# Mixture of experts on one core: three unequal lanes in the third pass, outputs scattered by assignment, first weights fetched during routing

## The reference

```python
choice = scores + router_bias                      # scores: sigmoid of a 64-wide product
_, top_e = lax.top_k(jnp.where(emask, choice, -jnp.inf), MOE_TOPK)     # 8 per token, from 4 of 8 groups
gw = gw / jnp.sum(gw, axis=-1, keepdims=True) * ROUTED_SCALE
...
def step(y, blk):                                  # blk: up to 128 tokens of one expert
    tok, wt, e = blk
    out = swiglu(hf[tok], exp_gate[e], exp_up[e], exp_down[e])         # 1024 -> 2 x 256 -> 1024
    return y.at[tok].add(out.astype(F32) * wt[:, None]), None
...
shared = swiglu(hf, sh_gate, sh_up, sh_down)
x = x + g2 * (y + shared); return rms_norm_2(x, final_g)
```

## Time and profile before

| | us |
|---|---|
| median of 3 runs (lowest, highest) | 2332.45 (2327.95, 2344.47) |
| profiled execution | 2335.72 |
| its span, first to last instruction | 2333.9 |
| PE busy in the span | 2148.9 (92%) |
| DVE busy | 1328.9 (57%) |
| POOL busy | 398.1 (17%) |
| DMA moved in the span | 446.34 MB, mean 191 GB/s |

### The profile page before, as it was taken

How to read it: one execution, slowest core, us unless ns; L and a number is a source line. 1 busy time by engine, 2 the same in 40 slices (tenths; PEclk the granted TensorE clock), 3 DMA queues, 4 the chain that set the end, 5 groups by cost and what they waited for, 6 DMA issues and landing times. The chain is left out here.

```text
span 2333.9 us, 27568 instructions
## 1 busy us (share of the span) xinstructions
PE 2148.9 (92%) x10379; PEld 1246.9 (53%) x10379; DVE 1328.9 (57%) x2524; ACT 461.0 (20%) x915; POOL 398.1 (17%) x771
## 2 busy tenths in 40 slices
PE   6999989999999999999879999998699999999976
PEld 3444654877785458883443788445333333333322
DVE  3448953766672134434968343535766767766756
ACT  2013561221110011004235232011011111111121
POOL 0005000112000000000000000000344444444524
PEclk9999999999999999999989999998899999999998
DMA  9412100545524015981111100401499989899977
GB/s 393 178 76 82 37 3 21 232 156 209 212 82 180 37 73 233 390 306 54 37 55 61 51 3 2 180 36 54 163 373 394 424 351 417 341 406 387 385 280 296
DMA packets 69142, 446.34 MB, mean 191 GB/s; under 512 B 12291, under 2 KB 12947, under 8 KB 44209
## 3 DMA queue, kind: packets, MB, share of 16 engines
q0 software_dynamic: 36176, 254.42, 27.2%
q1 hardware_dynamic: 32866, 190.52, 21.1%
HBM read 416.01 MB, written 73.45 MB: 210 GB/s over the span
## 5 line engine op out<-in xcount | busy, mean ns | idle before, releaser
L965 PE MATMUL psum<-arena 128*128 128x256 f32 x1904 | 416.3, 380 | 2.1 <-PEq L1005 2.1
L2824 PE MATMUL psum<-arena 128*64 128x512 f32 (+1 forms) x1088 | 367.4, 603 | 39.6 <-DVE arena L2872 16.8
L965 PEld LDWEIGHTS psum<-arena 128*128 128x128 f32 x1904 | 361.4, 190 | 62.3 <-issue 13.7
L2872 DVE STREAM_TRANSPOSE arena<-arena 32x256 f32<-32x256 f32 x832 | 362.2, 435 | 16.0 <-DMA arena<-scratch_h,arena 4.3
L2824 PEld LDWEIGHTS psum<-arena 128*64 128x64 f32 (+1 forms) x1088 | 144.7, 166 | 227.3 <-issue 201.4
L2815 PE MATMUL psum<-arena 128*64 128x512 f32 (+1 forms) x544 | 186.2, 598 | 1.2 <-ACT arena L2850 1.2
L1067 PE MATMUL psum<-arena 128*128 128x512 f32 x352 | 151.8, 592 | 0.3 <-PEq L1091 0.3
L2815 PEld LDWEIGHTS psum<-arena 128*64 128x64 f32 (+1 forms) x544 | 68.5, 163 | 113.2 <-issue 111.8
L869 PE MATMUL psum<-arena 128*128 128x512 f32 x256 | 113.7, 603 | 2.3 <-DVE arena L2432 1.5
L1067 PEld LDWEIGHTS psum<-arena 128*128 128x128 f32 x352 | 66.6, 190 | 83.4 <-issue 83.4
L2878 DVE COPY arena<-psum 128x512 f32<-128x512 f32 x51 | 35.3, 692 | 132.3 <-PE psum L2815 132.3
(11 more groups left out here) (520 smaller groups left out, 2925.3 us busy)
## 6 DMA issues: line engine op xcount, KB each, us to landing
scratch_expert_out<-arena SPq DMA_DIRECT2D x18, 2048.0 KB, 19.9
scratch_expert_out<-arena SPq DMA_DIRECT2D x51, 512.0 KB, 9.0
arena<-in_w_ada SPq DMA_DIRECT2D x12, 2048.0 KB, 16.2
arena<-in_ada_w POOLq DMA_DIRECT2D x12, 2048.0 KB, 8.8
arena<-in_w_up SPq DMA_DIRECT2D x22, 1024.0 KB, 4.8
arena<-in_w_in SPq DMA_DIRECT2D x9, 2048.0 KB, 10.8
arena<-in_w_down SPq DMA_DIRECT2D x5, 2048.0 KB, 8.3
arena<-in_w_o SPq DMA_DIRECT2D x2, 2048.0 KB, 8.5
```

The costliest lines, as they stand in the source:

```text
L965: last = pe.matmul(out, w[:, k, :], x[:, k, :], start=(k == 0), stop=(k == KH - 1))
L2824: last = pe.matmul(K.bank[2 + s][r, :], xt[:, s, P * k + r.start:P * k + r.stop], gu[:, lane, 2 * E_FF * k:2 * E_FF * (k + 1)], start=(k = ...
L2872: last = dve.transpose(channels[c:c + 32, :, a:a + 32], tokens[a:a + 32, :, c:c + 32])
```

## The change

The diff, cut to its core. The routing arithmetic on DVE is rewritten for three kinds of blocks (full; remainders of 33 to 64 rows; of 1 to 32 rows); it has about as many steps as before and is not shown but for the number of trips. `K.asg` lists the assignment of each row (token x 8 + rank), and `K.tok` comes from it by a shift, one more step at the end of the chain.

```diff
-LANES, LANE = 4, 32
+LANES, LANE = 5, 32
# phase_in2, sync: the fill of expert_out is gone
-                fill(3)
-            fill(len(parts))
-            sp.wait_ge(filled.sem, filled.n)
# phase_route, vector: ends = running sums of (full, 64-row, 32-row); RC_SHARE = 1, 2/3, 2/5; RC_TWOS = 0, 2, 4, ...
+            step(stt(out=num[:, 4:7], in0=ends[:, :, last], scalar=-0.5, in1=const[:, RC_SHARE:RC_SHARE + 3], op0=ALU.add, op1=ALU.mult))
+            step(dve.tensor_reduce(most, num[:, 4:7], AX.X, ALU.max))
+            step(ts(trips[:, :], const[:, RC_TWOS:RC_TWOS + LANE], most, None, ALU.is_lt))
+            step(dve.tensor_reduce(N, trips[:, :], AX.X, ALU.add))
# phase_route, gpsimd: after the sources are ready, first weights of three lanes and one down
+            for to, src, col_, landed in ((K.gu_lane[0], gu_rows, 0, K.gu_in[0]), (K.down_lane[0], down_rows, LANES, K.down_in[0]),
+                                          (K.gu_lane[1], gu_rows, 1, K.gu_in[1]), (K.gu_lane[2], gu_rows, 2, K.gu_in[2])):
+                offset = bass.IndirectOffsetOnAxis(ap=K.wrows[:, col_:col_ + 1], axis=0)
+                pool.indirect_dma_start(to, None, src, offset, bounds_check=EXPERTS * P - 1, oob_is_err=False).then_inc(landed.sem, 16)
...
# phase_experts
-    halves = lambda s: [(slice(0, P), s)] if s < 2 else [(slice(0, 64), 2), (slice(64, P), 3)]
+    tiles = lambda s: [(slice(0, P), s)] if s < 2 else [(slice(0, 64), 2), (slice(64, 96), 3), (slice(96, P), 4)]
# tensor: down product and gate/up product
                 for k in range(KD):
-                    for r, lane in halves(s):
+                    for r, lane in tiles(s):
                         last = pe.matmul(K.bank[2 + s][r, :], xt[:, s, P * k + r.start:P * k + r.stop],
-                                         gu[:, lane, 2 * E_FF * k:2 * E_FF * (k + 1)], start=(k == 0), stop=(k == KD - 1))
+                                         gu[lane][:, 2 * E_FF * k:2 * E_FF * (k + 1)], start=(k == 0), stop=(k == KD - 1))
# tensor, ahead of the loop: the first block's rows are turned here; ACT and DVE copy half each
+            pe.wait_ge(x_in[0].sem, 16)
+            for k in range(KD):
+                last = pe.transpose(K.bank[k // 4][:, P * (k % 4):P * (k % 4) + P], xg[:, 0, P * k:P * k + P], K.ident[:, :])
+            first_turned.by(last)
# gpsimd: no memset; down weights are fetched one step later than gate/up; a block is scattered four steps later
-            link(pool, pool.memset(xg[:, :, :], 0.0), cleared)
+            def scatter(i, s, off):
+                b = (s + off) % U
+                blocks_done(pool, out_act, i, s, off)
+                blocks_done(pool, out_dve, i, s, off)
+                pool.tensor_copy(out_rows[:, b:b + 1], K.asg[:, at(i, s + off)]).then_inc(out_step.sem, 1)
+                blocks_done(pool, out_step, i, s, off)
+                pool.tensor_tensor(wait_for[:, 6:7], K.rstd[:, 0:1], K.rstd[:, 0:1], ALU.add)
+                pool.indirect_dma_start(d["expert_out"], bass.IndirectOffsetOnAxis(ap=out_rows[:, b:b + 1], axis=0), out[:, b, :], None,
+                                        bounds_check=T * TOP - 1, oob_is_err=False).then_inc(out_dma[b].sem, 16)
...
+                gather(i, s, 1)
+                fetch_gu(i, s, lanes_of(s))
+                if not (isinstance(i, int) and U * i + s == U):
+                    fetch_down(i, s - 1)
+                if not isinstance(i, int) or U * i + s >= LAG:
+                    scatter(i, s, -LAG)
...
# sync: the plain store is gone; phase_combine: SP loads plain rows, all four tiles, no ring
-                dst = d["expert_out"][at(i, s)].rearrange("a p n -> (a p) n")
-                sp.dma_start(dst, out[:, s, :]).then_inc(out_dma[s].sem, 16)
+    ON_DVE, PARTS = 3, ((3, 5), (5, 8), (0, 3))
+            def load(t):
+                rows = d["expert_out"][P * TOP * t:P * TOP * (t + 1)].rearrange("(p j) n -> p j n", j=TOP)
+                for n, (lo, hi) in enumerate(PARTS):
+                    part_in[t][n].by(sp.dma_start(yg[t][:, lo:hi, :], rows[:, lo:hi, :]), 16)
```

More of the change, by code:

```diff
@@ L2613, in _ @@
             stt = dve.scalar_tensor_tensor
-            scan = lambda to, x: step(dve.tensor_tensor_scan(to[:, :], ones[:, :], x[:, :], 0.0, ALU.mult, ALU.add))
+            flat = lambda x: x.rearrange("p a e -> p (a e)")
             last = EXPERTS - 1
[L2616 to L2651, removed]
@@ L2660, in _ @@
[L2660 to L2664, removed]
+            N, most, widest = (num[:, m:m + 1] for m in range(3))
+            place_at, V, gone, found = num[:, 8:15], num[:, 15:16], num[:, 16:17], num[:, 17:18]
@@ new lines, in _ @@
+            V2, found2 = num[0:LANE, 18:19], num[0:LANE, 19:20]
+            full, fend, all_full = kinds[:, 0, :], ends[:, 0, :], ends[:, 0, last:]
+            step(tt(raised[:, :, :], cnt.unsqueeze(1).to_broadcast([P, 3, EXPERTS]), const[:, RC_UP:RC_UP + 3].unsqueeze(2).to_broadcast([P, 3, EXPERTS]), ALU.add))
+            step(ts(flat(raised[:, :, :]), flat(raised[:, :, :]), BLOCK.bit_length() - 1, None, ALU.logical_shift_right))
+            step(dve.tensor_copy(flat(kinds[:, :, :]), flat(raised[:, :, :])))
@@ new lines, in _ @@
+            step(dve.tensor_reduce(most, num[:, 4:7], AX.X, ALU.max))
+            step(ts(trips[:, :], const[:, RC_TWOS:RC_TWOS + LANE], most, None, ALU.is_lt))
+            step(dve.tensor_reduce(N, trips[:, :], AX.X, ALU.add))
+            step(stt(out=widest, in0=ends[:, 1, last:], scalar=all_full, in1=N, op0=ALU.subtract, op1=ALU.max))
+            vector = lambda m: const[:, RC_PLACE + 7 * m:RC_PLACE + 7 * m + 7]
+            step(stt(out=place_at, in0=vector(0), scalar=N, in1=vector(1), op0=ALU.mult, op1=ALU.add))
@@ new lines, in _ @@
+            step(stt(out=hat[:, :], in0=first_tail[:, :], scalar=at_(6), in1=got[:, :], op0=ALU.add, op1=ALU.add))
+            for m in (1, 2):
+                step(ts(got[:, :], first_tail[:, :], at_(m), at_(3 + m), ALU.is_gt, ALU.mult))
+                step(tt(hat[:, :], hat[:, :], got[:, :], ALU.add))
+            step(tt(base[:, :], fend, full, ALU.subtract))
+            step(tt(jump[:, :], hat[:, :], fend, ALU.subtract))
+            step(tt(jump[:, :], jump[:, :], tail[:, :], ALU.mult))
@@ L2686, in _ @@
             sf = slot_f[:, :, :].rearrange("p t j -> p (t j)")
[L2687 to L2696, removed]
+            step(stt(out=num[:, 20:28], in0=const[:, RC_BEYOND:RC_BEYOND + 8], scalar=N, in1=const[:, RC_BEYOND + 8:RC_BEYOND + 16], op0=ALU.mult, op1=ALU.add))
+            for lane in range(1, LANES):
+                to = again[:, 0:NT * TOP] if lane > 1 else beyond[:, :]
+                step(ts(to, sf, num[:, 19 + lane:20 + lane], num[:, 23 + lane:24 + lane], ALU.is_gt, ALU.mult))
+                if lane > 1:
+                    step(tt(beyond[:, :], beyond[:, :], to, ALU.add))
             link(dve, stt(out=K.slot[:, :], in0=sf, scalar=-1.0, in1=beyond[:, :], op0=ALU.add, op1=ALU.add), slots_done)
@@ L2813, in down_products @@
                     for k in range(2):
-                        for r, lane in halves(b):
+                        for r, lane in tiles(b):
                             last = pe.matmul(K.bank[5 + half][r, :], ht[:, b, P * k + r.start:P * k + r.stop],
-                                             down[:, lane, D * k + 512 * half:D * k + 512 * half + 512], start=(k == 0), stop=(k == 1))
+                                             down[lane][:, D * k + 512 * half:D * k + 512 * half + 512], start=(k == 0), stop=(k == 1))
                 last.then_inc(down_mm.sem, 1)
@@ L2909, in gather, with fetch @@
                                         bounds_check=T - 1, oob_is_err=False).then_inc(x_in[b].sem, 16)
-            def load(i, s, used, to, src, index, ready, landed_):
-                blocks_done(pool, used, i, s, -U)
+            def fetch(i, at, lanes, used, to, src, index, ready, landed_):
+                trip, last = at // U, lanes[-1] + 1
+                blocks_done(pool, used, i, at, -U)
                 pool.tensor_tensor(wait_for[:, 5:6], K.rstd[:, 0:1], K.rstd[:, 0:1], ALU.add)
-                for _, lane in halves(s):
-                    col_ = bass.ds(i + LANE * lane, 1) if not isinstance(i, int) else slice(LANE * lane + i, LANE * lane + i + 1)
+                for lane in lanes:
+                    n = LANE * lane + trip
+                    col_ = bass.ds(i + n, 1) if not isinstance(i, int) else slice(i + n, i + n + 1)
@@ L2916, in load @@
                     pool.tensor_copy(wrows[:, index + lane:index + lane + 1], K.source[:, col_]).then_inc(ready.sem, 1)
-                done = s + 1 if s < U - 1 else LANES
-                pool.wait_ge(ready.sem, LANES * i + done if isinstance(i, int) else i * LANES + done)
+                pool.wait_ge(ready.sem, LANES * (i + trip) + last if isinstance(i, int) else i * LANES + (LANES * trip + last))
```

(19 more changed lines are left out.)

220 lines of the change are left out of this document (130 added, 90 removed).

## The result

The changed kernel takes 2437.1 us (median of 4 runs, 2434.3 to 2438.1) against 2335.5: ratio 1.043, 95% interval 1.0409 to 1.0451. It is slower by 101.6 us, where 104 were forecast.

What follows compares the result with a forecast made beforehand. PE was taken to set the pace, with DMA nearly full. Fifteen trips of 45.9 us (689) replace 17 of 33.9 (576); with start, +2 and -6.5 at the end, +104 gives 2437 us, range 2280 to 2475.

Steps and rivals of the forecast that it cites:

- The deciding term: Third block: each width change costs 0.14 us and nothing overlaps across it; +13.4 us a trip.
- Trips: Expert loop: 15 trips instead of 17, at 45.9 us instead of 33.9; weight loads rise to 63.
- DMA and POOL under it: Expert loop: DMA's 42 us and POOL's at most 34 us a trip stay under 45.9; PE alone sets the pace.
- the 1.4 us: Expert loop: the time PE loses per trip in the kernel before, claimed to go once PE alone sets the pace.
- Start: Start of the expert stage: 2.4 + 4.2 us gained, some 6 us earlier; third block at 1698.
- 7.3 MB (17 us at 430) fit in: Routing: early weight transfers fit into DMA's idle time between 1641.9 and 1660 us.
- the sign named for the start: Expert stage: the start is right if the first gate/up begins about 1671.
- The terms that were named: Stage start: gather loses 2.7 us memset, gains 0.3 us step (2.4); turning the first rows takes 3 us, not 7.2 (4.2).
- End: After the last down product: scatter adds 2 us, plain loads bring the last stage's first join 6.5 us earlier.
- +2 and -6.5: Kernel's end: +2 us for the scatter's POOL work, -6.5 us for the first join at about 2283 through plain loads.
- Sum: Whole kernel: last down product at 2370 instead of 2262, everything moves by +104, span 2438, median 2437 us.
- The first rival: Third block: three widths run together at no price, DMA decides in front; 2293 us, chance 0.28.

Runs made afterwards that it cites:

- grouping: Changed kernel, third block taking all steps k of the 64-row lane first, then those of the two 32-row lanes: 2400.4 us, ratio 1.0268.
- 23.1 MB less: Changed kernel with lane 4's weights not moved from the third trip on: 2434.8 us, ratio to before 1.0432.
- mixed widths: Kernel before, with the second 64-row half of the third block as two tiles of 32 columns: 2533.5 us, ratio 1.0842.
- equal tiles: Changed kernel with the third block taken in four 32-column tiles: 2322.9 us, ratio to before 0.9943.
- the fill: Changed kernel with 8 of the 18 scratch fill transfers put back, and the wait at the end of SP's list: 2437.1 us, ratio 1.043.
- the three with less: Changed kernel without early weight fetch during routing (2446.4 us), with 5.2 of its 7.3 MB (2436.3), and the latter with four 32-column tiles (2323.3).

## Why the prediction was right

**The deciding term** was the third block, and it came out as worked: 16.0 and 8.0 us forecast, 15.95 and 8.01 measured, a change 0.14 against 0.134. The reason was right too, and not only the size: the same tiles without a second width lose it (2322.9), the kernel before gains it by a second width alone (2533.5), and grouping separates its two parts. The rule of the Trainium skill (TensorEngine Tiling (Array Packing), Key Properties) that a change of tiling mode drains the engine agrees with the weight loads of the changed kernel, where 32-column weights enter 1.0 us after the 64-column ones, when both passes are over.

**Trips.** 15, as counted; 45.4 us each, not 45.9. The working rounded a step of 1.98 to 2.0 and took 32.5 - 10.6 = 21.9 for the rest of a trip, which is 21.6: 6.6 us in 14 trips.

**DMA and POOL under it** cost nothing, as said: 23.1 MB less change nothing, and PE waits for no weights. What DMA cost the kernel before was read too small, though. Beside the 7.3 us of the earlier trace rows its view has

```profile
PE psum L2824 <- issue: 15.5, 9, 3.0
```

Nine third blocks began up to 3.0 us late there, with no releaser in the profile. With the 7.3 these are the 1.4 us that each of 16 trips lost. With mixed widths in that kernel, the same transfers under longer trips, its view of PE's waits has neither line. So the 15.5 were probably waits for weights too, but no row says so. The forecast doesn't hang on it, since it let the 1.4 us go.

**Start.** Forecast 6 us earlier; the first third block starts 4.8 earlier (1704.2 to 1699.4), and 2.2 of these are routing, whose last step ends at 1658.8 instead of 1661.1 and in the runs of this study anywhere from 1658.8 to 1667.4. From that step on it is 40.6 us instead of 43.1: 2.5. The step that failed is "7.3 MB (17 us at 430) fit in": they do not end with routing, and the stage waits for them, 5.43 us instead of 0.54. So the sign named for the start, a first gate/up at about 1671, did not come: it begins at 1674.0, as PE's timeline shows.

```profile
1671.15 1.97 PE L2840 MATMUL psum<-arena 128*128 128x128 f32 x8 [12.97 <-DMA arena<-scratch_h,arena]
1673.97 10.15 PE L2828 MATMUL psum<-arena 128*128 128x512 f32 x16 [0.85 <-DVE arena L2900]
```

The terms that were named came near: turning the first block takes 2.8 us instead of 7.2, as said, and from the stage's first step to the landing of the first rows it takes 6.9 us instead of 8.6, 1.7 less and not 2.4.

**End.** SP's timeline of the changed kernel, the first loads of the last stage:

```profile
2370.99 1.27 SPq L3051 DMA_DIRECT2D arena<-scratch_expert_out  x3
```

ACT's first step of that stage, in the changed kernel and then in the kernel before:

```profile
2371.01 5.95 ACT L3039 ACTIVATE arena<-arena 128x128 f32<-128x128 f32 x20 [1.86 <-PEq L2804]
...
2266.42 5.95 ACT L3018 ACTIVATE arena<-arena 128x128 f32<-128x128 f32 x20 [0.28 <-PEq L2802]
```

DVE's, its first sums and the first join:

```profile
2383.26 3.92 DVE L3021 SCALAR_TENSOR_TENSOR arena<-arena 128x1024 f32<-128x1024 f32 x3 [18.14 <-DMA arena<-scratch_expert_out]
2387.22 1.22 DVE L3024 TENSOR_TENSOR arena<-arena,psum 128x1024 f32<-128x1024 f32 x1
```

The last down product ends at 2364.3, so the first join comes after 22.9 us, where +2 and -6.5 on 27.6 make 23.1. The joins after it take 0.9 us more to the end than before, since DVE now waits 0.8 and 0.3 us for rows of the second and third tile. The split is near too: the stage opens 6.7 us after the last down product instead of 4.2, which makes +2.5, and its first join comes 16.2 us later instead of 23.4, -7.2. No run changes one of the two alone.

**Sum.** The span was forecast as 2438 and is 2432.2: -5.6 at the last third block, and everything behind it within 1 us. That the median meets the forecast to the microsecond is luck of 5 us: it lies 4.9 above this span, where the forecast allowed -1.5.

**The first rival** fell as a case (0.28) and was also priced wrong: its condition, three experts at full overlap, is the kernel with equal tiles, and that takes 2323, not 2293. The stretches of that kernel's front and of a part where PE waits:

```profile
1700.00:2050.00 350.00, 295.56 (x1326) 112.23 (x1324) 207.79 (x468) 32.63 (x78) 191.71 (x431) 0.93 1.00 416
...
1850.00:1900.00 50.00, 34.83 (x150) 13.11 (x150) 30.13 (x69) 3.90 (x10) 25.85 (x58) 0.87 1.01 425
```

DMA is saturated, as the rival had it, but at 416 GB/s over the front and not 427 (9 us on 150 MB), and it starts slowly: 204 GB/s from 1670 to 1675. The last six trips take 35.0 us each and not 33.9 (7 us). The last down product ends at 2253, not 2227. The rest of the 30 us wasn't taken apart, but for 4 that are the median above this profile's span.

The kernel with equal tiles is the fastest that computes everything: 12.7 us under the kernel before. Its loop gives less than half of that. By the two profiles (spans 2320.7 and 2333.9) the third block starts 3.4 us earlier, from there to the last down product it takes 5.7 us less, and the last stage 4.1 less.

## What to carry to other kernels

Give all tiles of TensorE that are to run side by side the same width, and split the wide one (its weights may be named twice) before adding a narrow one. Before packing more work into fewer trips, ask which resource the saved trips relieve: here, with the packing repaired, the bound went to the transfers, and the loop of 15 trips with 63 loads took only 5.7 us less than that of 17 with 58.

## What the runs showed of the hardware

- Four 32-column tiles, two of them with the same weights, take as long as two of 64 columns: 64 matmuls in a row of 7.08 us, 32 in one of 7.09.
- A stage whose predecessor issued indirect transfers on POOL began 2 to 3 us after all but a last few of their bytes had moved: the gap is 4.8 to 5.6 us in the six profiles with 7.3 MB, that of the fill among them, 0.5 in the three with less. What waits there, the chip or the program's own border between stages, isn't shown.
- With equal tiles the third block's gate/up group took 8.5 to 9.9 us, not 7.07, in the nine trips in which PE had waited 3.4 to 8.8 us for weights ahead of it; after shorter waits it took 7.07. One of the nine:

```profile
1772.82 9.60 PE L2829 MATMUL psum<-arena 128*32 128x512 f32 x64 [6.72 <-DMA arena<-in_exp_gu,arena]
```

  The granted clock is 0.87 in the second row of the fence on the first rival, a mix of its two levels, 2.4 and 1.2 GHz. The DMA share is 1.00 over that kernel's front, so the longer groups may have cost nothing there; no run tests it.
